# The low part of the fourth token sum: on GpSimd instead of VectorE, with a semaphore of its own

## The reference

```python
def modulate(x, g, shift, scale):
    return rms_norm(x, g) * (1 + scale) + shift

def swiglu(h, w_in, w_out):
    gate, up = jnp.split(h @ w_in, 2, axis=-1)
    return (jax.nn.silu(gate) * up) @ w_out

def ffn_half_step(xs, md, k, g, w_in, w_out):
    h = modulate(xs, g, md[3 * k], md[3 * k + 1])
    return xs + 0.5 * md[3 * k + 2] * swiglu(h, w_in, w_out)
```

## Time and profile before

| what | value |
|---|---|
| runs | 2494.91, 2492.38, 2494.68 us, median 2494.68 us |
| the profiled execution: its own time | 2494.53 us |
| its span, first to last instruction | 2492.7 us |
| TensorE busy | 2440.2 us, 98% of the span |
| VectorE busy | 1656.1 us, 66% |
| ScalarE busy | 919.9 us, 37% |
| GpSimd busy | 445.6 us, 18% |

### The profile page before, as it was taken

One profiled execution on the slowest core, in us unless ns is written; L12 is line 12 of the kernel. 1 busy time (PEld: TensorE's weight loads), 2 busy tenths in 40 slices (PEclk: granted clock), 3 DMA queues, 4 the chain that ended last, 5 costly groups with the idle time before them and its releaser, 6 DMA issues.

```text
span 2492.7 us, 40948 instructions
## 1 busy us (share of the span) xinstructions
PE 2440.2 (98%) x14641; PEld 2176.6 (87%) x14641; DVE 1656.1 (66%) x2612; ACT 919.9 (37%) x1458; POOL 445.6 (18%) x533
## 2 busy tenths in 40 slices
PE   7999999999899999999999999999999999999999
PEld 6888888888788888999899999999889988888887
DVE  6888678873888867757684747575876774643332
ACT  5333133331733322424442424243555563431221
POOL 2112111212211211000200000002666762000000
PEclk9999999999999999999999999999999999999999
DMA  7545435541154542222212222223011112433332
GB/s 232 162 145 167 133 114 148 160 129 41 35 169 139 168 130 72 73 68 63 72 52 72 72 59 81 63 68 93 26 51 37 39 34 68 127 99 95 93 107 87
DMA packets 367438, 239.51 MB, mean 96 GB/s; under 512 B 8081, under 2 KB 366066, under 8 KB 367346
## 3 DMA queue, kind: packets, MB, share of 16 engines
q1 hardware_dynamic: 366896, 238.12, 33.0%
q10 hardware_dynamic: 450, 0.18, 0.0%
HBM read 236.18 MB, written 2.10 MB: 96 GB/s over the span
## 4 chain that ended last, share of the span: by engine, by line
PE 75%; issue 13%; DVE 6%; POOL 3%; ACT 2%; DMA 1%; SPq 1%; POOLq 0%; DVEq 0%; ACTq 0%
PE pu L1502 46%; PE pu L1699 15%; PE pv L1892 5%; PE pu L1910 1%; PE pu L1544 1%; POOL ada_acc L858 1%; DVE h_lo L2500 1%; DVE xn L2493 1%; PE pu L1929 1%; PE pv L1920 1%; PE pu L1569 1%; PE pv L1544 1%; PE pv L1620 0%; POOL rr L898 0%; PE pv L1812 0%
## 5 line engine op out<-in xcount | busy, mean ns | idle before, releaser
L1502 PE MATMUL pu<-h_hi,w_hi 128*128 128x512 f32 (+1 forms) x1536 | 444.3, 352 | 5.3 <-DVE h_lo L2500 4.0
L1502 PE MATMUL pu<-h_lo,w_hi 128*128 128x512 f32 (+1 forms) x1536 | 442.4, 350 | 0.0
L1502 PE MATMUL pu<-h_hi,w_lo 128*128 128x512 f32 (+1 forms) x1536 | 442.2, 350 | 0.0
L2142 DVE TENSOR_TENSOR w_lo<-w_raw,w_hi 128x1024 fp32r<-128x1024 f32 (+3 forms) x208 | 277.8, 1337 | 173.4 <-ACT w_hi L941 167.4
L941 ACT ACTIVATE w_hi<-w_raw 128x1024 fp32r<-128x1024 f32 (+3 forms) x208 | 221.0, 1063 | 447.6 <-PE pu L1502 405.1
L2169 DVE SCALAR_TENSOR_TENSOR ada_acc<-ada_raw,cs,ada_acc 128x384 f32<-128x384 f32 x602 | 345.3, 615 | 11.2 <-DVE ada_acc L2169 2.0
L1502 PEld LDWEIGHTS pu<-h_hi,w_hi 128*128 128x128 f32 x1536 | 247.0, 188 | 47.7 <-issue 3.9
L1502 PEld LDWEIGHTS pu<-h_hi,w_lo 128*128 128x128 f32 x1536 | 248.0, 189 | 40.3
L1502 PEld LDWEIGHTS pu<-h_lo,w_hi 128*128 128x128 f32 x1536 | 247.0, 188 | 39.1
L858 POOL TENSOR_TENSOR ada_acc<-ada_acc,ada_parts 128x768 f32<-128x768 f32 x86 | 147.5, 1715 | 741.7 <-ACT ada_parts L948 686.9
L2393 DVE SCALAR_TENSOR_TENSOR xT<-pu,gate,xT 128x512 f32 (+3 forms) x142 | 84.4, 631 | 288.0 <-PE pu L1502 284.8
(11 more groups left out here) (320 smaller groups left out, 4998.4 us busy)
## 6 DMA issues: line engine op xcount, KB each, us to landing
ada_raw<-in_ada_w SPq DMA_DIRECT2D x86, 768.0 KB, 4.7
w_raw<-in_ffn_w_in SPq DMA_DIRECT2D x116, 512.0 KB, 4.0
w_raw<-in_ffn_w_out SPq DMA_DIRECT2D x40, 704.0 KB, 4.5
w_raw<-in_ffn_w_in SPq DMA_DIRECT2D x108, 256.0 KB, 3.0
w_raw<-in_diff_w_qkv SPq DMA_DIRECT2D x21, 512.0 KB, 5.2
w_raw<-in_ffn_w_out SPq DMA_DIRECT2D x24, 384.0 KB, 3.2
first_raw<-in_ada_w SPq DMA_DIRECT2D x8, 1024.0 KB, 11.8
w_raw<-in_ffn_w_out SPq DMA_DIRECT2D x24, 320.0 KB, 3.3
```

The costliest lines, as they stand in the source:

```text
L1502: last = pe.matmul(banks(ch, s_), w[:, j, :], r[:, SEG[s_]], start=(j == 0 and i == 0), stop=(j == k - 1 and i == 2))
L2142: dve.tensor_tensor(w_lo[:, ch, 0:k * P], w_raw[:, ch, 0:k * P], w_hi[:, ch, 0:k * P].bitcast(F32), ALU.subtract).then_inc(split_ready[ch], 1)
```

## The change

The subtraction that writes S4's lo part is taken out of VectorE's stream and put into GpSimd's, at two places: behind `granule_rests(1)` for block 1 and behind `sum_chunks(3)` for block 2. GpSimd waits for S4's hi part and for the sum, subtracts, and counts up a new semaphore `blk_s4`. TensorE waits for that semaphore before P3; its earlier wait on `blk_h` counts six lo parts per block instead of seven.

```diff
+            def last_sum_rest(z):
+
+                gp.wait_ge(blk_shi, 7 * z + 7)
+                gp.wait_ge(blk_sum, 16 * z + 16)
+                nc.gpsimd.tensor_tensor(s_lo[S4], s4_f32[:], s_hi[S4].bitcast(F32), ALU.subtract).then_inc(blk_s4, 1)
...
             granule_rests(1)
+            last_sum_rest(0)
             sum_chunks(3)
+            last_sum_rest(1)
             sum_chunks(4)
...
                     if sums:
-                        pe.wait_ge(blk_h, 7 * sums - 1)
+                        pe.wait_ge(blk_h, 6 * sums)
                     product(g, P6)
...
                     pe.wait_ge(blk_held, 2 * g + 2)
                     if sums:
-                        pe.wait_ge(blk_h, 7 * sums)
+                        pe.wait_ge(blk_s4, sums)
                     product(g, P3)
...
                 block_w_lo(g, P3)
-                if sums:
-                    dve.wait_ge(blk_shi, 7 * sums)
-                    dve.wait_ge(blk_sum, 16 * sums)
-                    dve.tensor_tensor(s_lo[S4], s4_f32[:], s_hi[S4].bitcast(F32), ALU.subtract).then_inc(blk_h, 1)
                 if not first:
                     block_prod(g - 1, 1)
                 block_w_lo(g, P4)
```

More of the change, by code:

```diff
@@ L418, in build @@
         blk_h = sem("blk_h")
+        blk_s4 = sem("blk_s4")
         aw_ready = sem("aw_ready")
```

## The result

| | median | runs |
|---|---|---|
| before | 2492.47 us (2487.87 to 2496.89) | 15 |
| changed | 2498.81 us (2495.69 to 2503.41) | 15 |
| ratio | 1.0021, 95% interval 1.0014 to 1.0028 | |

What follows compares the result with a forecast made beforehand. TensorE, 98% busy, was held to bound the kernel, stalling ahead of P3 through VectorE's order. 2494.53 + 1.29 + 1.30 = 2497.1 us, plus 3.0 for clock falls, gives 2500.1 us; range 2495.6 to 2501.8.

Steps and rivals of the forecast that it cites:

- What bounds the place: TensorE's stalls ahead of P3, 1.18 and 1.55 us: VectorE's order delays T2, then ScalarE's copy.
- Length of GpSimd's step: S4's lo subtraction of 1536 elements on GpSimd: 3.3 us of work and 0.3 of waiting.
- the straight line through the earlier trace alone: GpSimd's step length extended from shorter subtractions, 1.286 us for 512 elements and 2.355 for 1024: 3.42 us.
- Exclusion: GpSimd's subtraction and VectorE's `wx_lo` cannot overlap; `wx_lo` lasts about 3.6 us and ends 0.56 us after GpSimd's row.
- Delay per place: `wx_lo`, T2, the copy and P3 come late by 1.29 us in block 1 and 1.30 in block 2.
- Clock: TensorE's granted clock falls to 0.50 behind the longer stalls, losing 1.5 us each; bounds 0 and 3.0 us together.
- a fall at both places: Likeliest case: the clock falls behind both stalls ahead of P3, adding 3.0 us; 2500.1 us, chance 0.48.
- one-place falls: The clock falls behind only one of the two stalls ahead of P3: 2498.6 us, chance 0.15.
- overlap rival: GpSimd's step does not hold VectorE off; T2, limited by its load, starts 0.65 us earlier; 2493.2 us, chance 0.04.
- The forecast time: Whole kernel: base 2494.53 us plus delays at both places and 3.0 us for clock falls, 2500.1 us.
- allowance of 1.5 us for scatter: Whole kernel: the 1.5 us by which its runs differ, used to set the range's ends, 2495.6 and 2501.8 us.

Runs made afterwards that it cites:

- the fill: Changed kernel with GpSimd filling S4's lo place with zeros three times instead of subtracting; ratio 0.9995 to the kernel before.
- the two filled kernels: Changed kernel with 12 unread matmuls on TensorE ahead of the wait before P3 at both places, run twice; ratios 1.0007 and 1.0011 to the kernel before.
- c2_after: The changed kernel unaltered, one more trace to count falls of the clock; a single execution of 2492.91 us.
- e7_copy_u3_pool: Changed kernel with ScalarE's copy of P5's result and VectorE's `u_held` of P7 moved up; ratio 0.9997 to the kernel before.
- e8_first_only: The change in block 1 only, S4's lo part staying on VectorE in block 2; ratio 1.0009 to the kernel before.

## Why the prediction was right, point by point

- **What bounds the place.** Right. TensorE's stall is ScalarE's copy, that is T2, that is VectorE's order. With S4 left on VectorE, moving the copy and `u_held` takes the stall away with every amount of work unchanged.
- **Length of GpSimd's step.** Forecast 3.3 us of work and 0.3 of waiting; measured 3.65 us from 1017.38, of which VectorE held the first 0.29 (its row ends at 1017.67). That leaves 3.36 us of work, against 3.33 from the 2.26 us of the earlier trace rows and the slope of the earlier trace rows; the straight line through the earlier trace rows alone, 3.42, was 0.06 us too long.
- **Exclusion.** Right: `wx_lo` lasts 3.68 us instead of 0.69 and ends 0.55 us behind GpSimd's row, and beside the fill it lasts 0.69. That GpSimd's reading is the cause fits both, but a fill is also another kind of instruction, so this part is not shown. That the two engines share a pair of ports is told only by the Trainium skill ("SBUF — State Buffer", section "Who interferes with whom"); the 3.68 and 0.69 us agree with it. What would happen if `wx_lo` got in ahead of GpSimd's step was not seen: GpSimd's was first in all traces.
- **Delay per place.** Forecast 1.29 and 1.30 us; measured 1.30 to 1.33 and 1.26 to 1.28, from the distances without a fall; at place 2 these are only the two filled kernels. The stall itself at place 1 was forecast as 2.47 and was 2.50 in two traces and 2.80 in two, with the same distance where the clock did not fall (267.80 and 267.83 us): how early TensorE reaches the end of P7, against the mark, differs by 0.3 us between executions and costs nothing.
- **Clock.** The size was right: 1.55 us at place 1 (269.38 - 267.83), about 1.5 to 1.8 at place 2, against 1.5 forecast. The weak step is the one from the length of the stall to the fall. I took a fall at both places as the likeliest case and gave one-place falls only 0.15; the four traces show both, one, one, both. Stalls of 2.81 us at place 1 came with a fall and without, and so did stalls of 2.50; at place 2, which the prediction rightly held to be the surer one, the fall came every time. With the falls' share of six in eight, known only afterwards, the sum is 1.3 + 1.3 + 0.75 x (1.55 + 1.6) = 5.0 us, 0.20%, beside 1.0021 and 1.0024 measured. The forecast took 3.0 us for the falls and so was 0.6 us above the clock's average cost by these traces; that the time still came out near is in part luck.
- **The gain that could not come.** The overlap rival's bound, T2 held by its load, is confirmed: forecast 0.65 us per place, measured 0.78 and 0.33 without the step and 0.64 and 0.71 with the fill. (From the figures shown, 1014.84 + 3.1 is 1017.94, so the bound is 0.70 us; the prediction has 1017.99 and 0.65.)
- **The forecast time.** 2500.1 us against 2498.81. The median of before moved too, from 2494.68 of three runs to 2492.47 of fifteen. So two errors of different sign lie in the near hit: the forecast's base of 2494.53 was 2.1 us too high, and its difference of 5.6 us is 0.8 under the 6.3 between the medians. By the ratio, which is free of the base, 1.0022 was forecast and 1.0021 measured. The allowance of 1.5 us for scatter was taken from three runs; fifteen of the kernel before spread over 9 us.

## What to carry to other kernels

Before a step is moved to GpSimd because it is free, look at what VectorE runs at that moment. Here both subtractions read two tensors from SBUF, one waited for the whole of the other, and GpSimd's 3.65 us took the place of VectorE's 1.76 in front of everything that followed. Ask first what the stalled engine waits for: here it was not the amount of VectorE's work, but a copy queued behind a wait that it did not need, and by the distances reordering two instructions won 3.5 us where leaving the step out won 1.1. And measure a local change by the distance between two marks around it; here the five distances of place 1 with the changed kernel's delay and no fall agree within 0.04 us, while the medians of one and the same kernel differed by 3.6.

## What the runs showed that I had not expected

The clock's answer to one and the same stall changes from execution to execution: at place 1 it held behind 2.80 us in one trace and fell behind 2.50 us in another. A fall at these places lasts 3.4 us and cost 1.55 us at place 1. The kernel's times scatter also where nothing was changed: the start of S4's hi part in block 1, with the same work ahead of it, lay between 1009.16 and 1016.21 us in the traces. Falls are part of that, since the earliest trace, `c2_after`, has none ahead of this mark (granted clock 1.00 from 0 to 1009 us). They are not all of it: `e7_copy_u3_pool` has one fall there and reaches the mark at 1015.79 us, `e8_first_only` has two stretches at the low level and reaches it at 1014.68. The rest of the scatter stays open. And VectorE's waits for GpSimd are booked as busy time, in the row of the waiting instruction.
